# Norm weights applied at other places, the first loads in another order, and the first head's experts chosen in two passes

## What is computed

```python
xn  = rmsnorm(x, g_attn);  z = xn @ w_in          # w_in: 1024 x 2024, split into nine parts
c_q = rmsnorm(z[:, 0:384], g_q);  q = c_q @ w_uq  # g_q: 384 weights, w_uq: 384 x 768
c_kv = rmsnorm(z[:, 384:640], g_kv)               # and rope on the key columns
h   = x + [ MLA(q, c_kv) | DSA(...) ] @ w_out     # DSA adds a relative bias to its logits
xn2 = rmsnorm(h, g_ffn)
# PEER, 8 heads: two 128-key scores per head; top 16 of each; top 16 of their sums
s = einsum(xn2 @ w_pq, peer_keys);  sv, si = top_k(s, 16)
cv, ci = top_k(sv[0][:, None] + sv[1][None, :], 16);  eid = si[0][ci // 16] * 128 + si[1][ci % 16]
gate = softmax(cv);  act = gelu(peer_u[eid] . xn2)
y = rmsnorm(h + sum(gate * act * peer_v[eid]), g_final)
```

## Time and profile before

| | us |
|---|---|
| three runs | 1006.38, 1006.90, 1007.52; median 1006.9 |
| the profiled execution, its own time | 1008.4 |
| its span, first to last instruction | 1006.6 |
| PE, DVE, ACT, POOL busy | 728.6, 690.0, 401.9, 615.0 |
| mean granted TensorE clock | 0.839 |

### The profile page before, as it was taken

The page is one execution under the profiler, slowest core; times in us unless marked ns, Lnnn a source line. Parts: engine busy times, 40 slices in busy tenths (PEclk is TensorE's granted clock), DMA queues, the critical chain, the costliest instruction groups (busy, mean ns, idle before and its releaser), DMA issues.

```text
span 1006.6 us, 13868 instructions
## 1 busy us (share of the span) xinstructions
PE 728.6 (72%) x4233; PEld 366.8 (36%) x4233; DVE 690.0 (69%) x1729; ACT 401.9 (40%) x1152; POOL 615.0 (61%) x584
## 2 busy tenths in 40 slices
PE   8899997665878878866669866765586577564444
PEld 3476645221444536633213323322132244221101
DVE  2272956979687753699977698999964355667442
ACT  1163232323655771233324544653456343143322
POOL 0000476777777776476676776767776566677770
PEclk9899999788989989977767998789677788797555
DMA  9943599999999999999999999999999999999996
GB/s 344 335 160 120 204 386 410 412 413 409 411 409 408 402 412 398 403 413 381 349 361 390 406 406 408 406 405 404 409 404 407 411 415 418 412 409 409 405 410 267
DMA packets 122907, 381.01 MB, mean 379 GB/s; under 512 B 16106, under 2 KB 40762, under 8 KB 118226
## 3 DMA queue, kind: packets, MB, share of 16 engines
q0 software_dynamic: 83696, 304.81, 76.9%
q1 hardware_dynamic: 39042, 75.26, 20.1%
q10 hardware_dynamic: 96, 0.07, 0.0%
HBM read 377.90 MB, written 3.88 MB: 379 GB/s over the span
## 4 chain that ended last, share of the span: by engine, by line
DMA 28%; DVE 24%; PE 18%; POOL 15%; issue 8%; SPq 4%; ACT 3%; POOLq 0%; DVEq 0%
PE bank L471 12%; DMA rows<-in_peer_v,eid 11%; DMA rows<-in_peer_u,eid 9%; POOL rows L2023 6%; PE acc L471 5%; POOL rows L2041 5%; DVE rows L1479 5%; DMA wring<-in_w_in 3%; DMA x<-in_peer_u,eid 2%; SPq L2114 2%; DVE ql_t L1788 2%; DVE small L1787 2%; DMA z<-in_cache_kv 2%; DVE shared L1821 1%; DVE shared L1832 1%
## 5 line engine op out<-in xcount | busy, mean ns | idle before, releaser
L471 PE MATMUL acc<-rows,spread 128*64 128x512 f32 (+1 forms) x1124 | 327.9, 698 | 148.7 <-DMA rows<-in_peer_v,eid 119.8
L2023 POOL DMA_INDIRECT rows<-in_peer_v,eid x254 | 267.5, 1053 | 102.4 <-issue 70.1
L2041 POOL DMA_INDIRECT rows<-in_peer_u,eid x184 | 196.4, 1067 | 81.9 <-issue 49.4
L471 PEld LDWEIGHTS acc<-rows,spread 128*64 128x64 f32 (+1 forms) x1124 | 83.6, 154 | 318.4 <-issue 251.1
L1479 DVE CUSTOM_DVE_ANT_0 rows<-rows,xr_even 128x1024 f32<-128x1024 f32 x89 | 108.4, 1219 | 47.3 <-DMA rows<-in_peer_u,eid 46.5
L1479 DVE CUSTOM_DVE_ANT_0 rows<-rows,xr_odd 128x1024 f32<-128x1024 f32 x95 | 116.2, 1223 | 33.9 <-DMA rows<-in_peer_u,eid 33.3
L2041 POOL DMA_INDIRECT first_u<-in_peer_u,eid x37 | 40.3, 1090 | 101.0 <-DVE eid L1874 77.2
L471 PE MATMUL acc<-more_v,spread 128*64 128x512 f32 (+1 forms) x140 | 73.8, 722 | 22.3 <-DMA rows<-in_peer_v,eid 16.3
L1123 ACT ACTIVATE spread<-wide_consts,wts 128x64 f32<-128x64 f32 (+1 forms) x288 | 83.7, 338 | 4.7
L1114 ACT ACTIVATE gelus<-dots 128x2 f32<-128x2 f32 x144 | 28.6, 199 | 119.9 <-DVE dots L1479 119.4
L1116 ACT ACTIVATE wts<-gelus,gate 128x1 f32<-128x1 f32 x288 | 69.1, 287 | 4.7
(11 more groups left out here) (285 smaller groups left out, 1193.2 us busy)
## 6 DMA issues: line engine op xcount, KB each, us to landing
wring<-in_w_pq SPq DMA_DIRECT2D x12, 1024.0 KB, 8.8
z<-in_w_pq SPq DMA_DIRECT2D x5, 1024.0 KB, 8.7
wring<-in_cache_ckv SPq DMA_DIRECT2D x40, 128.0 KB
rows<-in_w_in SPq DMA_DIRECT2D x2, 2048.0 KB, 16.0
wring<-in_w_pq SPq DMA_DIRECT2D x2, 2048.0 KB, 12.5
wring<-in_w_out SPq DMA_DIRECT2D x4, 1024.0 KB, 10.3
wring<-in_cache_kv SPq DMA_DIRECT2D x32, 128.0 KB, 15.6
rows<-in_peer_v,eid POOLq DMA_INDIRECT x254, 13.6
```

Source lines behind the costliest of these rows:

```text
L471: return T.matmul(o, lhsT=l, rhs=r, start=start, stop=stop, skip_group_check=True)
L2023: nc.gpsimd.indirect_dma_start(out=v_ring[V_PLACE[n]], out_offset=None, in_=inp["peer_v"], in_offset=bass.IndirectOffsetOnAxis(ap=eid[t][: ...
L2041: nc.gpsimd.indirect_dma_start(out=u_ring[U_PLACE[n]], out_offset=None, in_=inp["peer_u"], in_offset=bass.IndirectOffsetOnAxis(ap=eid[t][: ...
```

## The change

Five edits in one:

1. The weight `g_q` is no longer multiplied in by DVE in `norms`; `cqn` is only scaled by the root. ACT multiplies it in when it copies the turned `cqn` out of PSUM, where the 384 columns are partitions: three copies of 128 x 128 with a scale for each partition in place of one of 128 x 384. `g_q` is loaded as 128 x 3.
2. `ropet`, `g_kv` and `uk_t` are loaded behind the fourth quarter of `w_in` and behind `w_uq`. The second half of `norms` (`ckv_nat` and the rope of one key part) becomes `latents`, for tile 0 behind `copies(0)`, and waits for these loads. PE's `heads_part(0)` waits for `w_uq_in` and for all three.
3. The first half of the first quarter of `w_in` is loaded as two transfers with a semaphore each.
4. POOL's copy `scr_d` waits for the fourth quarter of `w_in`.
5. The first head is chosen in two passes (`first_choice`): the best eight keys of each half give 64 sums (in 72 places, eight of them filled with a very small number), the best eight of these are located and written to `eid` and raise `slots_ready`; then come the next eight keys, all 136 candidates and the second eight. A new stop at slot 8 (`STARTS[0].insert(1, 8)`) makes POOL wait for them. The candidates lie in `shared`, no longer in `ql_t`.

The core of the diff:

```diff
 STARTS = [[16 * h for h, _ in p] for p in PARTS]
+STARTS[0].insert(1, 8)
+GIVEN = [sum(len(p) for p in STARTS[:t]) for t in range(3)]
...
-            pe.wait_ge(post_in, POST_IN)
+            pe.wait_ge(w_uq_in, 16)
+            pe.wait_ge(post_in, POST_IN)
...
-                copy(("cq", t), cq_t[:, :, 0:n], split(b[:, 0:3 * n], 3, n))
+                if t == 0:
+                    act.wait_ge(g_q_in, 16)
+                for j in range(3):
+                    copy(("cq", t), cq_t[:, j, 0:n], b[:, j * n:(j + 1) * n], j == 2, g_q[:, j:j + 1])
...
-                cq_ready.send(norm(z_q, g_q[0:n, :], cqn[0:n, :], 0), t)
-                norm(z_kv, g_kv[0:n, :], ckv_nat[0:n, t, :], 1)
+                cq_ready.send(V.tensor_scalar(cqn[0:n, :], z_q, small[0:n, 0:1], None, ALU.mult), t)
+
+            def latents(t):
+                n, zt = P[t], zs[t]
+                norm(zt[0:n, O_CKV:O_CKV + KVL], g_kv[0:n, :], ckv_nat[0:n, t, :], 1)
                 link(V, rope(t, zt[0:n, O_KR:O_KR + 1], 1, 32, kk[0:n, IDX:IDX + 1], 32))
...
+            def first_choice():
+                b = ready(dve, ("sc", "a", 0))
+                score = [b[:, 128 * j:128 * j + 128] for j in range(2)]
+                keys = [sc[:, j, :] for j in range(2)]
+                for j in range(2):
+                    i = V.max(sv[:, j, 0:8], score[j])
+                link(V, i)
+                for j in range(2):
+                    i = V.max_index(si_u[:, j, 0:8], sv[:, j, 0:8], score[j])
+                V.tensor_tensor(first_cand[:, 0:8], free(sv[:, 0, 0:1], (0, 8)), sv[:, 1, 0:8], ALU.add)
+                link(V, V.tensor_tensor(first_cand[:, 16:72]..., ALU.add))
+                pick_eight(0, 72)
+                locate(0, 8)
+                V.match_replace(out=first_cand[:, 0:72], ..., imm_value=TAKEN)
+                for j in range(2):
+                    i = V.match_replace(out=keys[j], in_to_replace=sv[:, j, 0:8], in_values=score[j], imm_value=TAKEN)
+                drained(i, ("sc", "a", 0))
...
+                pick_eight(8, STAIR)
+                V.tensor_tensor(gt[:, 0, :], cv[:, 0, :], ..., ALU.subtract).then_inc(gate_sub, 1)
+                locate(8, 16)
+                share_gates(0, 0)
...
             x_turned(1)
-            dve.wait_ge(norm_in, NORM_IN)
             read_done(dve, ("z", 1, 0))
             norms(0)
             x_turned(2)
             read_done(dve, ("z", 2, 0))
             link(V, copies(0))
+            dve.wait_ge(post_in, POST_IN)
+            latents(0)
...
-                        best_keys(t, 0, 1, ("sc", "a", 0))
-                        ready(dve, ("pq", "b", 0))
-                        choose(t, 0, lambda: None)
+                        link(V, V.memset(first_cand[:, 8:16], TAKEN))
+                        first_choice()
...
+            pool.wait_ge(lodge_in[3], 16)
             nc.gpsimd.dma_start(scr_d, ...).then_inc(scr_d_out, 16)
...
-                    load(lodge[0][:, 0:2048], inp["w_in"][:, 0:2048], w_in_half)
+                    load(lodge[0][:, 0:1024], inp["w_in"][:, 0:1024], w_in_quarter)
+                    load(lodge[0][:, 1024:2048], inp["w_in"][:, 1024:2048], w_in_half)
...
-            for o, i in norm_consts:
-                load(o, i, norm_in)
+            load(g_q[:, :], inp["g_q"], g_q_in)
             lodge_columns("in", 3)
+            load(w_uq[:, :, :], inp["w_uq"], w_uq_in)
```

More of the change, by code:

```diff
@@ L126, in build @@
         g_fin = sb("g_fin_sb", [128, DM])
-        g_q = sb("g_q_sb", [128, QL])
+        g_q = sb("g_q_sb", [128, 3])
         g_kv = sb("g_kv_sb", [128, KVL])
@@ L1573, in post @@
                     norms(t)
+                    latents(t)
                 link(V, rope(t, zt[0:n, O_KI:O_KI + 1], 1, 32, kk[0:n, 0:1], 32))
@@ L1885, in choose @@
                 link(V, i)
-                pause()
+            def first_choice():
[8 more added lines that the diff above has]
+                V.tensor_tensor(first_cand[:, 0:8], free(sv[:, 0, 0:1], (0, 8)), sv[:, 1, 0:8], ALU.add)
+                link(V, V.tensor_tensor(first_cand[:, 16:72].rearrange("p (a b) -> p a b", b=8), free(sv[:, 0, 1:2], (1, 7), (0, 8)),
+                                        free(sv[:, 1, 0:1], (0, 7), (1, 8)), ALU.add))
+                pick_eight(0, 72)
+                locate(0, 8)
+                V.match_replace(out=first_cand[:, 0:72], in_to_replace=cv[:, 0, 0:8], in_values=first_cand[:, 0:72], imm_value=TAKEN)
+                for j in range(2):
+                    i = V.match_replace(out=keys[j], in_to_replace=sv[:, j, 0:8], in_values=score[j], imm_value=TAKEN)
+                drained(i, ("sc", "a", 0))
+                read_done(dve, ("sc", "a", 0))
+                for j in range(2):
+                    i = V.max(sv[:, j, 8:16], keys[j])
+                link(V, i)
+                for j in range(2):
+                    V.max_index(si_u[:, j, 8:16], sv[:, j, 8:16], keys[j])
+                V.tensor_tensor(first_cand[:, 72:STAIR].rearrange("p (a b) -> p a b", b=8), free(sv[:, 0, 8:9], (1, 8), (0, 8)),
+                                free(sv[:, 1, 0:1], (0, 8), (1, 8)), ALU.add)
+                i = V.tensor_scalar(first_cand[:, 8:16], sv[:, 1, 8:16], sv[:, 0, 0:1], None, ALU.add)
+                link(V, i)
+                pick_eight(8, STAIR)
+                V.tensor_tensor(gt[:, 0, :], cv[:, 0, :], free(cv[:, 0, 0:1], (0, PTOP)), ALU.subtract).then_inc(gate_sub, 1)
+                locate(8, 16)
+                share_gates(0, 0)
@@ new lines, in pick_eight, with locate @@
+            def pick_eight(first, w):
+                k = slice(first, first + 8)
+                link(V, V.max(cv[:, 0, k], first_cand[:, 0:w]))
+                link(V, V.max_index(ci[:, 0, k], cv[:, 0, k], first_cand[:, 0:w]))
+            def locate(first, m):
+                k = slice(first, first + 8)
+                for half, step in enumerate((1024.0, 128.0)):
+                    V.scalar_tensor_tensor(out=placed[:, half, 0:m], in0=iota16[:, 0:m], scalar=step, in1=si_u[:, half, 0:m],
+                                           op0=ALU.mult, op1=ALU.add)
+                link(V, V.tensor_scalar(pa[:, 0, k], ci[:, 0, k], 0x1F8, 7, ALU.bitwise_and, ALU.logical_shift_left))
+                V.scalar_tensor_tensor(out=pb[:, 0, k], in0=pa[:, 0, k], scalar=2048.0, in1=pa[:, 0, k], op0=ALU.is_ge, op1=ALU.mult)
+                link(V, V.tensor_scalar(pa[:, 0, k], pa[:, 0, k], 1024.0, 0.0, ALU.subtract, ALU.max))
+                link(V, V.scalar_tensor_tensor(out=pb[:, 0, k], in0=ci[:, 0, k], scalar=128.0, in1=pb[:, 0, k], op0=ALU.mult, op1=ALU.subtract))
+                for half, (place, e) in enumerate(((pa, ea), (pb, eb))):
+                    o = first_hot[:, 128 * half:128 * half + 8 * m].rearrange("p (k c) -> p k c", c=m)
+                    link(V, V.tensor_tensor(o, free(place[:, 0, first:first + 1], (1, 8), (0, m)),
+                                            free(placed[:, half, 0:1], (0, 8), (1, m)), ALU.bitwise_xor))
+                    link(V, V.tensor_reduce(out=e[:, k], in_=o, axis=AX.X, op=ALU.min))
+                for j, q in SPREAD[0]:
+                    i = V.scalar_tensor_tensor(out=eid[0][WIDE * q:WIDE * q + WIDE, first + j:first + 8:PAIR],
+                                               in0=ea[WIDE * j:WIDE * j + WIDE, first + q:first + 8:PAIR], scalar=float(KEYS),
+                                               in1=eb[WIDE * j:WIDE * j + WIDE, first + q:first + 8:PAIR], op0=ALU.mult, op1=ALU.add)
+                i.then_inc(slots_ready, 1)
@@ L2060, in _ @@
             load(g_turned[:, :], inp["g_attn"], first_in)
-            norm_consts = [(ropet[:, :, :], cst["rope"]), (g_q[:, :], bcast(inp["g_q"], QL)), (g_kv[:, :], bcast(inp["g_kv"], KVL))]
-            post_consts = [(w_uq[:, :, :], inp["w_uq"]), (uk_t[:, :, :], inp["w_uk"])]
-            assert 16 * len(norm_consts) == NORM_IN and 16 * len(post_consts) == POST_IN
+            post_consts = [(ropet[:, :, :], cst["rope"]), (g_kv[:, :], bcast(inp["g_kv"], KVL)), (uk_t[:, :, :], inp["w_uk"])]
+            assert 16 * len(post_consts) == POST_IN
             consts = [(g_ffn_turned[:, :], inp["g_ffn_turned"]), (wide_c[:, :], cst["wide"]), (short_c[:, :], cst["short"]), (g_ffn[:, :], bcast(inp["g_ffn"], DM)),
@@ L2320, in laid_out @@
     a["w_pq"] = columns(a["w_pq"][0])
+    a["g_q"] = a["g_q"].reshape(3, 128).T
     a["w_uk"] = a["w_uk"][0].reshape(KVL, HR, 128).transpose(2, 1, 0)
```

19 lines of the change are left out of this document (14 added, 5 removed).

## The result

The change made the kernel **slower**: 1015.98 us (median of 6 runs, 1012.34 to 1018.57) beside 1007.59 for the kernel before (6 runs, 1006.38 to 1008.68), ratio 1.0082, 95% interval 1.0063 to 1.0100. Forecast were 998.8, a range of 996.0 to 1003.5, and 0.05 for slower, by another mechanism than the one that acted.

A forecast was written before the change was run, and what follows sets the result against it. DMA bytes were taken as the bound from 116 us, a chain of dependent work before that. Terms -6.71 + 0.25 - 1.66 = -8.1 us took the median 1006.9 to 998.8 us, range 996.0 to 1003.5.

The forecast's parts named there:

- another mechanism than the one that acted: Slower case: `scr_d` copy and read-back take twice as long, `bias_d` lands at 86.4, DVE stands still; 1020 us, chance 0.05.
- Constants, fourth quarter, clock (-6.71): PE's fourth-quarter product of `w_in`: starts 4.02 us sooner and runs 2.69 us shorter, together 6.71 us gained.
- The slow clock that was booked as 2.69: PE's fourth-quarter product: at full clock with no idle time ahead, 6.70 us instead of 9.39, 2.69 gained.
- Moved constants 0: PE's `heads_part(0)` and DVE's `latents(0)`: the later loads land by 41.3, just in time; cost 0, range 0 to 3.
- stores +0.25: ACT ahead of the first exponential: z's stores on SP's queue land near 59.5, losing 0.25 us, up to 2.5.
- bias table 0: POOL's later copy and read-back of `bias_d` end about 58.1, wanted after 59.7; cost 0.
- The three rivals of lateness: SP-queue loads late (1001.8 us, 0.20); fourth quarter held by its queue (1005.2, 0.08); `bias_d` late (1020, 0.05).
- Two passes: First head's choice: first gather 3.2 us sooner against the scores, of which 1.66 us lasts at slot 6.
- bring nothing that lasts: Rival: slot 6 or the dot products hold POOL, so the two-pass choice gains nothing; 1000.4 us, chance 0.11.
- `g_q` on ACT: ACT's three copies for one cost some tenths more, hidden by the fourth-quarter product and the full DMA stage.
- the first term, -6.71: PE's fourth-quarter product of `w_in` ends at 41.7 instead of 48.4, 6.71 us gained.
- each microsecond by which the unbroken stream starts earlier should come off the end: DMA stage from 116 us: its bytes stay the same, so an earlier start shortens the total equally.

The follow-up runs named there:

- the zeros: Kernel before with large targets at multiples of 256, plus 40 products by a zero tile in PE's waits ahead of tile 1's heads: 991.93 us, ratio 0.9850.
- the whole change with the same zeros: All five edits, large targets at multiples of 256, plus 40 products by a zero tile in PE's waits ahead of tile 1's heads: 988.54 us, ratio 0.9835.
- the old addresses: Changed kernel with `g_q`'s tile 384 columns wide again, so tiles behind it lie as in the kernel before: 1002.62 us, ratio 0.9959.
- the first part at the old addresses: Changed kernel without the two-pass choice of the first head, tiles placed as in the kernel before: 1002.87 us, ratio 0.9956.
- the clock held: Whole change and kernel before, both with targets at multiples of 256 and 40 zero products in PE's waits: 988.54 and 991.93 us, ratios 0.9835 and 0.9850.

## Why the prediction was wrong, point by point

The sum was set against one execution of the kernel before. Seven traces have its instructions up to the first scores, and they do not agree on the fourth quarter. First its product in two others (all targets at multiples of 256, without and with the zeros), for 9.39 us from 39.01 in the earlier trace rows; then the first scores on DVE, 104.03 in the earlier trace rows, in the second of these and in the whole change with the same zeros:

```profile
38.39 6.81 PE L474 MATMUL bank<-wring,xt 128*128 128x488 f32 x16 [1.00 <-DMA wring<-in_w_in]
38.28 8.10 PE L477 MATMUL bank<-wring,xt 128*128 128x488 f32 x15 [0.94 <-DMA wring<-in_w_in]
102.42 0.50 DVE L1828 MAX8 shared<-bank 128x8 f32<-128x128 f32 x2 [0.67 <-PE bank L477]
97.89 0.50 DVE L1925 MAX8 shared<-bank 128x8 f32<-128x128 f32 x2 [0.54 <-PE bank L481]
```

- *Constants, fourth quarter, clock (-6.71): right in mechanism, too large in size.* The start came at 35.71 for 34.99 forecast and the product took 6.73 for 6.70, so the forecast of the changed kernel holds. What it was set against does not. In the seven traces the product starts at 38.1 to 39.0 and `heads_part(0)` behind it at 45.1 to 48.2, median 46.6; the execution that the sum started from is the last of them. In the ten traces with the new order `heads_part(0)` starts at 41.4 to 42.5, median 42.1. So the term is about 4.6, and the first scores tell the same, medians 102.42 and 97.75, 4.7 us. The slow clock that was booked as 2.69 costs less in the other six, and in the first line above next to nothing.
- *Moved constants 0, stores +0.25, bias table 0: right in what they add.* `heads_part(0)` began at 42.28 and `latents(0)` at 36.56 without a wait; the first exponential came at 60.13 for 59.7; `bias_d` was there at 65.31. The stores did hold ACT for 2.03 us, until 58.61, but what the first exponential waited for last was DVE's reduction, so the 0.25 is met by another cause. The three rivals of lateness did not occur.
- *Two passes: right at slot 6, void at the end.* From the first scores to slot 6 it is 18.6 us in every trace without them and 17.1 in every trace with them: 1.46 us, 1.66 forecast. At the old addresses 0.8 of it is left at the 96th gather and 0.4 at the 144th, and nothing is measured in the time. The rival "bring nothing that lasts" was right, its place was not: not slot 6 or the first dot products. Where it goes differs from pair to pair of traces; it was not found.
- *The step that failed first* is "`g_q` on ACT": it priced the copies' tenths, and nothing else of that edit. The tile's new size moved all the tiles behind it. With the rest of the change that costs 12.5 us (4.1 below the kernel before at the old addresses, 8.4 above it at the new ones), in the kernel before 10.7. It is no term of the sum and no rival.
- *The step that failed second* is the size of the first term, -6.71, taken from a single execution: it measured about 4.7. By the medians of the traces the stream starts 4.7 + 1.46 = 6.1 us earlier at slot 6, not 8.1. The sum took the 1.5 us by which that execution lay above the median off its time; its scores came 1.6 later than the median of the seven, so the same lateness was probably counted as a gain as well.
- *The step that failed third* is "each microsecond by which the unbroken stream starts earlier should come off the end". For the first part at the old addresses it holds as far as the runs can tell, 4.7 of 4.7. With the passes it does not: 4.1 of 6.1, at multiples of 256 about 2 (1.8 by the medians, 2.2 by the ratios), and there with the clock held 3.4 or 1.5. A DMA share of 1.02 from 116 to 1000 us hides that the rate at that share is not fixed (391 to 410 GB/s in one window), and that from 250 to 350 us the stream can hang on the heads of tile 1, where a low clock of PE and waits of POOL come together in most traces.

What stays open: which executions lose the head start, where the 1.46 us of the passes go, and why no more than half or so of the 6.1 comes off the time even with the clock held. One profile a kernel does not tell this; the first gather alone stands at 112.85 and at 109.83 in two kernels whose instructions are the same and whose addresses differ.

## What to carry to other kernels

An edit that changes a tile's size also moves every tile allocated behind it: compare the start addresses, modulo 256 bytes, of all targets of transfers before and after, and put them at multiples of 256 where there is room (here 256 bytes of padding gave 1.3%, three times what the whole change gave at the addresses of before). Before a cost is read off a trace as what a change will save, read it in more than one execution: here the one at hand was the latest of seven, by 1.6 us of a forecast 6.5. Before a gain in an early stage is booked against a DMA-bound one, look in that stage for a place where the transfers wait for an engine; a DMA share of 1 averaged over 900 us does not exclude it. And when a trace moves the same bytes at the same share more slowly, look at how the bytes lie before looking at when they move.

## What the runs showed of the hardware that was not expected

- A shift of `wring` and the tiles behind it by 32 or 64 bytes off a multiple of 256, with or without the gathers' rings, costs 10.7 to 12.0 us in 1007. From 550 to 700 us the DMA section counts 10.09 MB for SP's queue and 50.63 for the gathers in the kernel before, 9.96 and 48.57 in the changed one, at 20.1% and 83.6% against 20.5% and 83.3% of the engines' time: the gathers' packets became slower by 3.9% a byte as well, though from 850 to 970 us, nearly without pages, they did not (within 0.2%). With `wring` and what follows moved and the rings left in place it is 4.3% (48.77 MB at 84.0%). Why pages that lie badly slow the gathers beside them was not found.
- From 450 to 550 us, where SP loads `in_cache_kidx` into the same tiles, the rate is 370 and 371 GB/s at the two addresses: in that stretch no loss is seen.
- Rings of gathers 64, 96 or 128 bytes above a multiple of 256 gave 409 GB/s alike; at a multiple, 419.
- With products of zeros in PE's waits but for one of 3.05 us ahead of tile 1's heads, the granted clock was 1.00 from 200 to 240 us and 0.50 from 242 to 246, behind that wait. With zeros in that wait as well, which left 1.38 us of it, it stayed at 1.00 to 248.
